# Token rows of the first expert layer made by one-hot products on TensorE in place of indirect gathers

## What is computed

```python
def _hier_moe(h, w_group, b_group, w_router, b_router, w_gate, w_up, w_down):
    # every token picks one of 4 groups and 2 of its 8 experts: eid, wts
    # assignments are sorted by expert and laid out in blocks of rows
    xb = h_pad[tok_buf].reshape(n_blocks, MOE_BLOCK, d)
    def expert_block(args):
        xe, e = args
        return (jax.nn.silu(xe @ w_gate[e]) * (xe @ w_up[e])) @ w_down[e]
    y = lax.map(expert_block, (xb, blk_e)).reshape(cap, d)
    return jax.ops.segment_sum(y * w_buf[:, None], tok_buf, num_segments=t + 1)[:t]
```

## Time and profile before

| | |
|---|---|
| three runs, us | 2398.14, 2401.6, 2402.22 |
| median, us | 2401.6 |
| span of the profiled execution, us | 2400.5 |
| TensorE busy / weight loads | 2173.3 us (91%) / 1361.6 us (57%) |
| DVE / ACT / POOL busy | 1108.4 / 692.3 / 215.8 us |
| bytes moved by DMA | 656.73 MB, mean 274 GB/s |
| share of the chain that ended last | TensorE 12%, DMA 10%, DVE 3%, ACT 1% |

### The profile page before, as it was taken

One profiled execution on the slowest core, in us unless ns is written; L12 is line 12 of the kernel. 1 busy time (PEld: TensorE's weight loads), 2 busy tenths in 40 slices (PEclk: granted clock), 3 DMA queues, 4 the chain that ended last, 5 costly groups with the idle time before them and its releaser, 6 DMA issues. The chain is left out here.

```text
span 2400.5 us, 29499 instructions
## 1 busy us (share of the span) xinstructions
PE 2173.3 (91%) x11404; PEld 1361.6 (57%) x11404; DVE 1108.4 (46%) x1760; ACT 692.3 (29%) x1102; POOL 215.8 (9%) x330
## 2 busy tenths in 40 slices
PE   7999999998899999988898888888788899999996
PEld 5778788876777888856633333333366533333332
DVE  5677655465676456577511111111587522222223
ACT  4243344344334443366111110110237111111110
POOL 2000000010000001100111111111120000000000
PEclk9989999999999999999799999998889899999998
DMA  8745576573655657501799999999830799999995
GB/s 295 260 151 190 193 235 202 184 277 135 226 206 193 211 171 248 163 2 39 301 335 401 411 409 411 406 408 411 302 84 8 299 380 428 428 428 429 428 428 230
DMA packets 175600, 656.73 MB, mean 274 GB/s; under 512 B 16295, under 2 KB 61943, under 8 KB 150288
## 3 DMA queue, kind: packets, MB, share of 16 engines
q1 hardware_dynamic: 159648, 622.65, 67.6%
q0 software_dynamic: 14032, 30.00, 4.0%
q10 hardware_dynamic: 1824, 2.73, 0.3%
HBM read 649.97 MB, written 23.79 MB: 281 GB/s over the span
## 5 line engine op out<-in xcount | busy, mean ns | idle before, releaser
L750 PE MATMUL bank<-sb_ring_rounded,sb_hT_rounded 128*128 128x512 f32 x2432 | 605.7, 397 | 18.7 <-DVE sb_ring_rounded L2045 8.4
L1382 PE MATMUL bank<-sb_ring,sb_arena 128*64 128x512 f32 x1984 | 491.1, 640 | 94.1 <-DMA sb_ring<-in_w_up 91.3
L750 PEld LDWEIGHTS bank<-sb_ring_rounded,sb_hT_rounded 128*128 128x128 f32 x2432 | 459.4, 191 | 119.5 <-issue 12.9
L1382 PEld LDWEIGHTS bank<-sb_ring,sb_arena 128*64 128x64 f32 x1984 | 152.4, 146 | 378.7 <-issue 372.9
L2045 DVE TENSOR_TENSOR sb_ring_rounded<-sb_ring,sb_ring_rounded 128x2048 fp32r<-128x2048 f32 (+1 forms) x142 | 314.9, 2258 | 112.4 <-ACT sb_ring_rounded L1516 107.4
L750 PE MATMUL bank<-sb_ring_rounded,sb_arena_rounded 128*128 128x512 f32 x1408 | 356.8, 395 | 7.6 <-DVE sb_arena_rounded L2032 7.0
L1516 ACT ACTIVATE sb_ring_rounded<-sb_ring 128x2048 fp32r<-128x2048 f32 x146 | 268.1, 1887 | 125.7 <-PE bank L750 100.1
L750 PEld LDWEIGHTS bank<-sb_ring_rounded,sb_arena_rounded 128*128 128x128 f32 x1408 | 266.1, 190 | 63.3 <-DVE sb_arena_rounded L2032 7.3
L1926 ACT ACTIVATE sb_hb<-bank 64x512 f32<-64x512 f32 x64 | 37.8, 590 | 697.4 <-PE bank L1382 697.4
L1406 PE MATMUL bank<-sb_ring,sb_arena 128*64 128x512 f32 x1008 | 233.4, 606 | 3.5 <-DVE sb_arena L2877 3.5
L2877 DVE COPY sb_arena<-bank 128x256 f32<-128x256 f32 x64 | 27.1, 424 | 319.2 <-PE bank L1393 319.1
(11 more groups left out here) (372 smaller groups left out, 2121.9 us busy)
## 6 DMA issues: line engine op xcount, KB each, us to landing
sb_ring<-in_w_down SPq DMA_DIRECT2D x63, 2048.0 KB, 22.0
sb_ring<-in_w_up SPq DMA_DIRECT2D x62, 2048.0 KB, 21.3
sb_ring<-in_w_gate SPq DMA_DIRECT2D x62, 2048.0 KB, 16.9
sb_ring<-in_w_ada SPq DMA_DIRECT2D x48, 1024.0 KB, 7.5
sb_ring<-in_ffn_w_gu SPq DMA_DIRECT2D x44, 1024.0 KB, 7.8
sb_ring<-in_xa_w_kv SPq DMA_DIRECT2D x16, 1024.0 KB, 7.3
sb_ring<-in_ffn_w_down SPq DMA_DIRECT2D x16, 1024.0 KB, 6.4
sb_ring<-in_od_w_in SPq DMA_DIRECT2D x12, 1024.0 KB, 7.7
```

The lines of the kernel that those rows point to most:

```text
L750: ins = pe.matmul(bank[b][0:rows, :], rnd(x), rnd(w[:, k, :]), start=start and k == k0 and q == 0, stop=stop and k == k1 - 1 and q == len( ...
L1382: ins = pe.matmul(bank[2 * j + part][part * ROWS:(part + 1) * ROWS, :], mxT[:, j, k, :], w[:, k, :], start=k == 0, stop=k == KD - 1)
```

## The change

- Layer 0 brings its rows in as layer 1 does: `mark`, `place_rows` and `turn_placed` now take the layer. The store of the tokens to DRAM, the gathers, `turn_rows`, `turned_rows`, and the table of token indices go, and with them SP's wait for `rows0`.
- With 512 tokens the one-hot matrix has four tiles. `mark` makes it in two halves and writes it rounded (fp32r) into `sb_silu` and `sb_fix`, which are free by then. The products are fp32r. To keep the tokens exact, each is split: ACT writes a rounded copy (`token_rounded`) into a new tensor `sb_tokens` (three tiles) and `bc` slot 0 (the fourth), and DVE subtracts it from the token (`token_rest`) to leave the remainder. `place_rows` has 2 halves x 4 tiles x 2 parts = 16 products for each pair in layer 0; layer 1 keeps its 4 float32 products.
- Four small DVE operations that give the place numbers, and `mark(0)`, now also stand in layer 0's `route`; the first `place_rows` stands ahead of the products for the index table.
- Layer 0 gets single buffers for `mact` and `mup`, as layer 1 has, and its output rows go to `hb` and `bc` slot 1. So the two fills of `bc` slots 0 and 1 for layer 1 move from ahead of the loop into POOL's last pair (`next_modulation`), behind its wait for the rows loaded back.
- The SBUF kept for POOL's DMA descriptors is cut by `dynamic_dma_scratch_size=4096`; before, it had its default.

```diff
-        by_rows = ["places", "equals", "marked"] if l else ["rows0", "rows1", "picked_in"]
...
+        def my_of(l, j, own=False):
+            if l == 1:
+                return view(6144, 2, D)[0:ROWS, j, :]
+            return tokens[0:ROWS, j, :] if own else hb[0:ROWS, 0, :] if j == 0 else bc[0:ROWS, 1, :]
...
-                if l == 0:
-                    sp.wait_ge(m["rows0"], 16)
-                else:
+                if l == 1:
                     fetch(0, 2, 2)
                 fetch(1, 2, 2)
...
-                if l == 1:
-                    claim(T0)
-                    claim(T1)
-                    place_rows(0)
+                claim(T0)
+                claim(T1)
+                if l == 0:
+                    pe.wait_ge(s["tok_lo"], tiles)
+                place_rows(l, 0)
...
+                    cols = slice(half * NB, (half + 1) * NB)
+                    if l == 0:
+                        for t in range(4):
+                            for part, v in enumerate((token_high(t), hr[:, t, :])):
+                                ins = pe.matmul(bank[T0 + half], rnd(marks_of(t)), rnd(v[:, cols]), start=t + part == 0, stop=t + part == 4)
...
-                        if l == 0 and not (last and j == 1):
-                            turn_rows(1 - j, e + 1, i + 1 + j)
-                        if l == 1 and not last:
-                            (place_rows, turn_placed)[j](i + 1)
+                        if not last:
+                            (place_rows, turn_placed)[j](l, i + 1)
...
+                def token_rounded(t):
+                    act.activation(rnd(token_high(t)), hr[:, t, :], ACT.Copy).then_inc(s["tok_hi"], 1)
...
+                for half in range(2):
+                    at = flat[:, 8 * half:8 * half + 8].unsqueeze(2).to_broadcast([P, 8, ROWS])
+                    if half:
+                        dve.wait_ge(m["equals"], i * 3 + 2)
+                    dve.tensor_tensor(equal, row, at, ALU.is_equal).then_inc(m["equals"], 1)
+                    dve.wait_ge(m["equals"], i * 3 + 2 * half + 1)
...
+                    dve.tensor_tensor(rnd(to), place_marks[:, :, 0, :, :], place_marks[:, :, 1, :, :], ALU.add)\
+                       .then_inc(m["marked"] if half else m["equals"], 1)
...
+            def token_rest(t):
+                dve.wait_ge(s["tok_hi"], t + 1)
+                dve.tensor_tensor(rnd(hr[:, t, :]), hr[:, t, :], whole(token_high(t)), ALU.subtract).then_inc(s["tok_lo"], 1)
...
-                        if l == 1 and j == 0 and not last:
-                            mark(i + 1)
+                        if j == 0 and not last:
+                            mark(l, i + 1)
...
-                pool.indirect_dma_start(out=mx[0:ROWS, j, :], out_offset=None, in_=DR["tok"],
-                                        in_offset=bass.IndirectOffsetOnAxis(ap=at, axis=0),
-                                        bounds_check=tiles * P - 1, oob_is_err=False).then_inc(m[f"rows{j}"], 16)
...
+                    if l == 0 and last and j == 1:
+                        pool.wait_ge(m["pe_xT"], i * 4 + 2)
+                        apart()
+                        next_modulation()
                     if not (opening(i) and j == 0) and not (own and j == 1):
-                        store(1 - j, i * 2 + j - 1)
+                        store(1 - j, i * 2 + j - 1, last and j == 1)
```

More of the change, by code:

```diff
@@ L1330, in route, with place_rows @@
                         pe.wait_ge(*c.next(s["marks_ready"]))
-                    ins = pe.matmul(bank[S1][0:ROWS, 0:BLK * N_EXP], rnd(mrow[:, q, :]), rnd(mcols[l][:, q, :, :]), start=q == 0, stop=q == 2 * tiles - 1)
+                    ins = pe.matmul(bank[S1][0:ROWS, 0:BLK * N_EXP], rnd(mrow[:, q, :]), rnd(mcols[l][q // tiles][:, q % tiles, :, :]), start=q == 0, stop=q == 2 * tiles - 1)
                 publish(ins, S1, "d")
-            def place_rows(i):
-                m = moe[1]
+            def place_rows(l, i):
+                m = moe[l]
                 pe.wait_ge(m["marked"], i + 1)
@@ L1373, in experts @@
                 for b in range(8):
-                    if l == 0 or b not in (T0, T1):
+                    if b not in (T0, T1):
                         claim(b)
@@ L1908, in y_lo @@
                     since(act, m["my_free"], e - 1)
-                    act.activation(my[0:ROWS, j, 0:NB], bank[S0][0:ROWS, :], ACT.Copy).then_inc(m["y_lo"], 1)
+                    act.activation(my_of(l, j)[:, 0:NB], bank[S0][0:ROWS, :], ACT.Copy).then_inc(m["y_lo"], 1)
                 def y_both(j, e):
@@ L1921, in pair @@
                         e = i * 2 + j
-                        more = not (last and j == 1)
                         act.wait_ge(m["pe_hidden"], e + 1)
@@ L1926, in pair @@
                         act.activation(msil[0:ROWS, j, :], bank[2 * j][0:ROWS, :], ACT.Silu).then_inc(m["silu"], 1)
-                        if l == 0 and more:
-                            turned_rows(1 - j, e + 1)
-                        if l == 1 and not last:
+                        if not last:
                             (rows_out, placed_turned)[j](i + 1)
@@ L2058, in ahead, with norm @@
                     split(n + 1)
-            def norm(tiles, gain, shift=None, stored=None, lo=LO2, turn=True, meanwhile=None):
+            def norm(tiles, gain, shift=None, lo=LO2, turn=True, meanwhile=None):
                 settle()
-                for i, t in enumerate(tiles):
-                    if stored:
-                        dve.wait_ge(s[f"tok_stored{i}"], stored)
                 inv_rms(tiles)
@@ L2809, in route @@
                 hot = monehot[:, 0:T, :, :]
-                for t in range(0, T, T // 2):
-                    choose(t, t + T // 2)
+                choose(0, T // 2)
+                if l == 0:
+                    for t in range(3):
+                        token_rest(t)
+                choose(T // 2, T)
                 e4 = st[:, 32:32 + 4 * T].rearrange("p (t g) -> p t g", g=4)
                 dve.tensor_tensor(rnd(mtmp[:, 0:T, 0:N_EXP]), hot[:, :, 0, :], hot[:, :, 1, :], ALU.add).then_inc(*c.up(s["marks_ready"]))
+                if l == 0:
+                    token_rest(3)
                 take(S0)
@@ L3031, in _, with experts @@
                 experts(l)
-        def experts(pool, c, step, l):
+        def experts(pool, c, l, next_modulation):
             m = moe[l]
             tiles = 4 - 2 * l
-            if l == 0:
-                for q in range(2):
-                    pool.wait_ge(*c.next(s[f"tok_stored{q}"], 16 * tiles // 2))
             pool.wait_ge(*c.next(s["idx_ready"]))
@@ L3082, in pair @@
                     for j in range(2):
-                        pool.tensor_copy(own_row[:, j:j + 1], column(0, i * 2 + j)).then_inc(s["own_rows"], 1)
+                        pool.tensor_copy(own_row[:, j:j + 1], column(i * 2 + j)).then_inc(s["own_rows"], 1)
                 for j in range(2):
-                    if l == 0 and not last:
-                        gather(j, i * 2 + j + 2)
                     if not opening(i):
```

187 lines of the change are left out of this document (79 added, 108 removed).

## The result

The changed kernel takes 2367.81 us (median of 4 runs, 2364.79 to 2370.35) against 2399.87 us before (2397.01 to 2402.22): a ratio of 0.9866, 95% interval 0.9852 to 0.988. The forecast was 2371 us. The profiled execution of the changed kernel has a span of 2365.9 us.

A forecast was written before the change was run, and what follows sets the result against it. The weight stream was taken to bound both expert loops. Layer 0's last `hidden` comes 30.6 us earlier, its end adds 0: 2400.5 - 30.6 = 2369.9 of span, plus 1.1 for the median, 2371 us; range 2364 to 2386.

The forecast's parts named there:

- The bound and the 1.20 us: Expert loops: weight stream bounds both; layer 0 slower by 1.20 us per expert: gather 0.28 + 0.68, store 0.11, unplaced 0.13.
- The rule against it: DMA queues: transfers interleave on the same 16 engines, so a gather costs only its bytes; the change returns 0.28 us.
- The cover: Layer 0 pairs: TensorE needs 27.2 us, transfers 30.2, so 3.0 us of each pair cover the products.
- the queue empty for 13 us in all: First six experts of layer 0: SP's waits leave the weight queue empty for 13 us; first to last `hidden` 452.5.
- The first `hidden`: Start of layer 0: first `hidden` at 1203.5 us, 2.5 earlier; bounds 1202.5 and 1207.2.
- Routing: Layer 0 routing: `token_rest` operations fall into DVE's waits for logits and ranks; taken at nothing, up to 4 us otherwise.
- The end of layer 0: Behind the last `hidden`: later fills and earlier stores taken as even, 0; bounds -3 and +6 us.
- rival B: Start and end of layer 0: first products at lower clock (+3.7) and late fills (+6) give 2381 us; chance 0.11.
- The descriptor space: POOL's smaller descriptor space: costs nothing in the loop and elsewhere; can only add to the end of layer 0.
- A (2393): Layer 0 loop: dips stay, belonging to larger stores or other traffic; 15.91 us per expert, 2393 us; chance 0.10.
- C (2488): Layer 0 pairs: rounded products take as long as float32 ones, 0.91 us each, TensorE becomes the bound; 2488 us; chance 0.05.
- D (2399): Layer 0 stream: held back by the turn of the homes, not gathers; stays at 16.2 us, 2399 us; chance 0.03.

The follow-up runs named there:

- the empty gather: Kernel before, with the bound of its gathers from the third expert on set to row 0, so at most one row of each moves: 2370.33 us, ratio 0.988.
- the wide rows: Kernel before, each gather from the third expert on replaced by a plain transfer of 960 bytes into each of 128 partitions: 2371.16 us, ratio 0.9884.
- gathers given back: Changed kernel plus, from the fifth expert on, a gather per expert from another tensor into SBUF that nobody reads: 2401.53 us, ratio 1.0003.
- the run with early fills: Changed kernel with POOL's two modulation fills ahead of its wait for the loaded rows of tiles 0 and 1, last pair: 2370.94 us, ratio 0.9883.

## Why the prediction was right, step by step

**The bound and the 1.20 us.** Right. The stream sets the pace in both layers, 0.68 us of the difference went with the gathers beyond their bytes, and it came back with them: 15.05 us per expert, 15.10 forecast (bounds 14.99 to 15.23). Measured as one thing, a gather costs 1.14 us, 0.18 more than my 0.96; the 0.13 that I couldn't place was the gather's, and 0.05 that I had given to the store. The larger store costs 0.06 (15.05 - 14.99) where I took 0.11. Its bytes flow out of SBUF, and the runs show no loss beyond them for these stores.

**The rule against it.** That transfers of all queues interleave on the same engines and cost their bytes holds here for the empty gather and nearly for the wide rows. For rows heaped on few partitions it is off by a factor of 3 to 5.

**TensorE's products.** The size was right: 0.228 us for one, 3.65 for sixteen, 27.4 for a pair. The cover, 3.0 us per pair forecast and 2.7 measured (30.1 - 27.4), is there from the fifth pair on. In the first four it isn't, and the step "the queue empty for 13 us in all" was too small: first to last `hidden` took 454.9 us, 2.4 more than forecast, at a stream that was faster than forecast; it should have saved 1.4 there. So the early gaps cost about 4 us more than I walked out. Two runs agree: without the products and the gathers the same stretch takes 450.8 us, and with half the products 449.7.

**The first `hidden`.** Forecast 1203.5, measured 1200.93, in an execution that was 3.8 us ahead long before the routing. Against that the step was too optimistic: from the start of the mark to `hidden` it took 12.67 us (1188.26 to 1200.93), 11.0 forecast, because most of the first products ran at the lower clock, 1.2 GHz: from 1190.86 to 1196.33 us the granted clock is 0.69, and the products start 0.43 us apart at first and 0.23 at the end. The way from them to `hidden` is not the rows' but the pair count's: the products of the index table stand behind them on TensorE, DVE waits 2.97 us for these, and the count is ready at 1199.58, when the turned rows have been copied since 1198.92. TensorE reads the count before its first `hidden`. I had this as a bound (7.4 us for the sixteen; it became 5.47). With half the products the same way took 10.84 us.

**Routing.** Right: three `token_rest` fill the wait for the logits, and the second half of the choice starts at 1180.31, right behind them, and the last logits are ready at 1180.26.

**The end of layer 0.** 0 forecast, +0.6 measured, which is no more than profiles of the same fills differ by: with gathers given back this stage takes 35.62 us, with half the products 35.74, as before the change (35.67). The fill is late for DVE by 3.09 us, but taking that wait away gains nothing: the run with early fills loses at the loads, and at the stores behind them, what it gains at the fills. The late fill of rival B is there; its price isn't.

**The descriptor space.** Wrong: "nothing" was 4 us, a ratio of 0.9983 (0.9972 to 0.9994), in the kernel before, and 6.05 us lie at the end of the spans. I had looked for waits of POOL for space, found none, and not considered that it could touch the end of the program.

**The sum.** The likeliest value was 3 us too high, and that it came so near was partly luck. The forecast's stages, at the spans: last `hidden` 30.6 us earlier, measured 30.8. But 3.8 of this lie ahead of everything that the forecast priced, so the start and the loop gave about 27; 6 came from the end, and 2.2 were lost behind layer 0's last `hidden` (0.6 there and 1.6 in layer 1, where these runs' profiles differ by up to 6 us among themselves). A gain 3.6 us smaller than forecast, one of 6 us that wasn't forecast and a loss of 2.2 cancelled.

**The rivals.** A (2393) is refuted by both ends: without gathers no dips, with them all of them. B (2381) is at +0.6 and +1.8 of its 9.7 us. C (2488) is refuted by 0.228 us per product; its mechanism is real: at twice the work, as if a product took 0.46, TensorE becomes the bound and the kernel takes 2394.3, 26.5 of the 32 us gone. By that run the pace of the stream is lost from (30.1 - 23.7) / 16 = 0.40 us per product on, and not from 0.56, which I had set at the old pace of 32.4. D (2399) is refuted by 15.05.

## What to carry to other kernels

A small transfer beside a saturated stream isn't priced by its bytes: if it heaps whole rows on few partitions while the stream fills all of them, it can cost three to five times as much, and spreading it over all partitions in short pieces takes most of that back. Read it from the profile as a rate that falls by more than the transfer moves, and test it by moving the same bytes elsewhere. A slack per loop step holds only where the loop is already limited by the other side: count the first steps, which live on buffers filled ahead, apart. And look at what lies behind the last operation of a profile, too.

## What the hardware showed unexpectedly

0.12 MB of 4 KB rows cost 0.84, 1.01 or 1.56 us of stream time by the partitions they went to, and 0.39 us as 960-byte pieces in all 128; out of SBUF, stores of 0.128 MB per expert (3.08 MB in 24) cost 0.06 us more than layer 1's of 0.075 MB. Beside rows that went in, the weights' own packets took up to 0.93 us per expert longer. A gather with (nearly) all of its rows out of bounds cost 0.05 us. With 4096 bytes of descriptor space the kernel before was 4 us faster, and every profile with this space lacked some 5.7 us at its end in which the others record nothing; two with the large space lacked them as well.
